# Combining expert outputs: gates applied at the exit from PSUM, and gathers that add onto x inside the DMA

## What is computed

```python
def rms_norm(x, g):
    y = x * rsqrt(mean(x * x, axis=-1) + 1e-6)
    return y * g

for layer in range(2):
    h = rms_norm(x, norm_mix_g[layer])
    x = x + mixer[layer](h)
    h = rms_norm(x, norm_ffn_g[layer])
    x = x + hier_moe(h, ...)
return rms_norm(x, norm_final_g)

def hier_moe(h, ...):            # of each token: 2 experts, each with a gate
    ...
    gate = softmax(top_v) * p_g[:, None]
    expert = g_sel[:, None] * 8 + top_i
    ...
    def expert_block(xb, e):
        return (silu(xb @ w_gate[e]) * (xb @ w_up[e])) @ w_down[e]
    ...
    y = zeros_like(t).at[tok_sorted].add(ybuf[dest] * gate_sorted[:, None])
```

## Time and profile before

| what | us |
|---|---|
| median of 3 runs | 1822.61 (1816.19 to 1827.16) |
| the profiled execution | 1822.49 |
| its span, first to last instruction | 1820.7 |
| VectorE busy in the span | 541.3 |
| TensorE busy in the span | 1421.9 |
| GpSimd busy in the span | 166.1 |

### The profile page before, as it was taken

The page is one execution under the profiler, slowest core; times in us unless marked ns, Lnnn a source line. Parts: engine busy times, 40 slices in busy tenths (PEclk is TensorE's granted clock), DMA queues, the critical chain, the costliest instruction groups (busy, mean ns, idle before and its releaser), DMA issues. The chain is left out here.

```text
span 1820.7 us, 18610 instructions
## 1 busy us (share of the span) xinstructions
PE 1421.9 (78%) x7013; PEld 685.3 (38%) x7013; DVE 541.3 (30%) x1109; ACT 247.1 (14%) x501; POOL 166.1 (9%) x211
## 2 busy tenths in 40 slices
PE   6998757968977877877848977894988878868872
PEld 3443745543333333322313456653333323323330
DVE  6998596231110110110123157324111101101014
ACT  2201322111000000000001035311100000000001
POOL 0007250001000000000010000000000000000002
PEclk9999977978998998998987989995998988988996
DMA  6512405247999999999984200406999999999995
GB/s 227 171 37 29 33 13 217 84 187 286 388 396 399 397 401 403 400 397 404 405 347 154 93 1 1 186 35 266 341 374 405 395 395 402 389 393 407 396 419 189
DMA packets 75026, 494.38 MB, mean 272 GB/s; under 512 B 14704, under 2 KB 21488, under 8 KB 50016
## 3 DMA queue, kind: packets, MB, share of 16 engines
q1 hardware_dynamic: 53984, 440.23, 62.5%
q0 software_dynamic: 9472, 32.32, 5.7%
q10 hardware_dynamic: 11520, 21.15, 3.1%
HBM read 465.88 MB, written 27.79 MB: 271 GB/s over the span
## 5 line engine op out<-in xcount | busy, mean ns | idle before, releaser
L565 PE MATMUL psum<-ring,work 128*64 128x512 f32 x992 | 501.7, 665 | 162.3 <-DMA ring<-in_moe_w_up 159.5
L566 PE MATMUL psum<-ring,work 128*64 128x512 f32 x992 | 502.4, 666 | 0.0
L565 PEld LDWEIGHTS psum<-ring,work 128*64 128x64 f32 x992 | 147.5, 153 | 489.5 <-issue 486.1
L578 PE MATMUL psum<-ring,work 128*64 128x512 f32 x992 | 226.6, 599 | 31.4 <-DVE work L716 31.4
L713 DVE TENSOR_TENSOR work<-work,psum 64x512 f32<-64x512 f32 x64 | 44.1, 690 | 681.9 <-ACT work L670 608.0
L670 ACT ACTIVATE work<-psum 64x512 f32<-64x512 f32 x64 | 37.8, 590 | 879.0 <-PE psum L566 879.0
L566 PEld LDWEIGHTS psum<-ring,work 128*64 128x64 f32 x992 | 147.5, 153 | 0.0
L578 PEld LDWEIGHTS psum<-ring,work 128*64 128x64 f32 x992 | 66.7, 137 | 145.2 <-issue 125.3
L719 DVE COPY work<-psum 128x512 f32<-128x512 f32 x64 | 44.3, 692 | 247.9 <-PE psum L578 247.9
L1495 PE MATMUL psum<-ring,hT 128*128 128x512 f32 x256 | 112.1, 600 | 2.1 <-ACT work L1614 2.1
L862 POOL COPY ints<-ints 64x1 uint32 (+1 forms) x64 | 11.4, 178 | 864.3 <-PE psum L557 816.0
(11 more groups left out here) (341 smaller groups left out, 1415.9 us busy)
## 6 DMA issues: line engine op xcount, KB each, us to landing
ring<-in_moe_w_gate SPq DMA_DIRECT2D x62, 2048.0 KB, 17.7
ring<-in_moe_w_up SPq DMA_DIRECT2D x62, 2048.0 KB, 24.1
ring<-in_moe_w_down SPq DMA_DIRECT2D x62, 2048.0 KB, 24.0
y_dram<-work ACTq DMA_DIRECT2D x128, 128.0 KB, 9.0
ring<-in_hyb_w_in SPq DMA_DIRECT2D x5, 2048.0 KB, 9.7
ring<-in_swa_w_qkv SPq DMA_DIRECT2D x3, 2048.0 KB, 17.9
y_dram<-ones POOLq DMA_DIRECT2D x1, 4096.0 KB, 19.9
ring<-in_hyb_w_out SPq DMA_DIRECT2D x2, 2048.0 KB, 10.6
```

The source lines that it names most:

```text
L565: nc.tensor.matmul(bank[2 + b][0:BLK, :], XT[b][:, c, :], g[:, c, :], start=c == 0, stop=c == KC - 1)
L566: i = nc.tensor.matmul(bank[2 + b][BLK:P, :], XT[b][:, c, :], u[:, c, :], start=c == 0, stop=c == KC - 1)
L578: i = nc.tensor.matmul(bank[6 + b][BLK * hf:BLK * (hf + 1), :], HTE[b][:, c, :], d[:, c, hf * HALF:(hf + 1) * HALF], start=c == 0, stop=c ...
```

## The change

1. The token-number product goes to a second table `BL2`, and `BL1` stays a plain one-hot table of blocks. VectorE multiplies `BL1` with the gates (128x384), and TensorE multiplies places with it into PSUM bank 5, once for each half of the partitions: 16 more matmuls. VectorE copies the result, a gate for every row of every block, to `SLG` (128x48).
2. `dve_y` is a multiplication by the column of `SLG` that belongs to the block, instead of a copy. Inside the loops the column's number is in a register. The rows in `y_dram` are now already times their gates.
3. The 8 gathers go straight onto x: `compute_op=ALU.add` makes the DMA add the row that it fetches onto `xv[:, t, :]`. The order is k=0 of the four tiles, then k=1 of the four tiles, and each of the last four waits until the k=0 gather of the same tile has landed.
4. The 8 multiply-adds of VectorE per layer, the buffers `YK` and the semaphore `x_new` are gone; ScalarE's norm and SyncE's loads wait for the k=1 gathers themselves.

```diff
--- before.py
+++ after.py
@@ -217,7 +217,6 @@
         dve_own, act_own, pool_own = Count("dve_steps"), Count("act_steps"), Count("pool_steps")
         n_sq, n_ms, n_rt, n_h, n_hp, n_ea, n_ed = (Count(n) for n in (
             "norm_squares", "norm_mean", "norm_root", "norm_rows", "norm_transposed", "norm_evac_act", "norm_evac_dve"))
-        x_new = Count("x_updated")
         p_tr, p_ev, c_tr, c_ev = (Count(n) for n in ("s5_rows_transposed", "s5_rows_out", "s5_c_transposed", "s5_c_out"))
         sc_a, sc_b = Count("s5_dve_to_act"), Count("s5_act_to_dve")
         u_mm, u_ea, u_tr, u_ev = (Count(n) for n in ("u_proj", "u_evac", "u_transposed", "u_ready"))
@@ -316,7 +315,6 @@
         HD = [WK[0:BLK, 12288 + 512 * b:12800 + 512 * b] for b in range(2)]
         HTE = [cut(WK, 13312 + 256 * b, 256).rearrange("p (c n) -> p c n", c=HC) for b in range(2)]
         YE = [cut(WK, 13824 + 512 * b, 512) for b in range(2)]
-        YK = [cut(WK, 1024 * i, 1024) for i in range(8)]
 
         W2 = [cut(WK, 4096, SLOT), cut(WK, 0, SLOT), HT[:, :]]
         RT0 = 14848
@@ -350,12 +348,15 @@
         assert 20 + MAXOV + 2 <= 64
         ONES = sb("ones", P)
         gates = rt("gates")
+        BL2 = cut(WK, 12288 + 8 * NBLK, 8 * NBLK)
+        SLG = rt("big")[:, 0:NBLK]
 
         g_lg, g_ex, g_exr, g_A, g_C, g_idx, g_zero, g_wr = (Count(n) for n in (
             "router_logits", "router_to_act", "router_exp", "router_onehots", "router_counts", "router_indices",
             "ones_set", "router_weights_joined"))
         h_st = sem("h_stored")
         g_L, g_Lm, g_sl = Count("router_places"), Count("router_lists_mm"), Count("router_lists")
+        g_G, g_Gm = Count("router_gate_places"), Count("router_gate_lists_mm")
         xg_ld = [sem(f"x_block{b}") for b in range(2)]
         e_stg, e_xt, e_xe, e_gu, e_a, e_h, e_ht, e_he, e_dn, e_y = (sem(n) for n in (
             "blk_index", "blk_x_transposed", "blk_x_evac", "blk_gate_up", "blk_silu", "blk_hidden", "blk_h_transposed",
@@ -388,10 +389,17 @@
             i.then_inc(g_C.s, 1)
 
             pe.wait_ge(g_L.s, l + 1)
-            pl, bl = shp(PL1, 8, BLK), shp(BL1, 8, NBLK)
+            pl, bl, bg = shp(PL1, 8, BLK), shp(BL2, 8, NBLK), shp(BL1, 8, NBLK)
             for a in range(8):
                 i = nc.tensor.matmul(bank[2][0:BLK, 0:NBLK], pl[:, a, :], bl[:, a, :], start=a == 0, stop=a == 7)
             i.then_inc(g_Lm.s, 1)
+
+            pe.wait_ge(g_G.s, l + 1)
+            for hf in range(2):
+                for a in range(8):
+                    i = nc.tensor.matmul(bank[5][BLK * hf:BLK * (hf + 1), 0:NBLK], pl[:, a, :], bg[:, a, :], start=a == 0,
+                                         stop=a == 7)
+            i.then_inc(g_Gm.s, 1)
 
         def act_router(act, l, A_):
             act.wait_ge(g_ex.s, 2 * l + 1)
@@ -524,13 +532,15 @@
             V(tv.tensor_tensor(rt("ob"), rt("ob"), rt("ei"), ALU.add))
             V.sync()
             V(tv.scalar_tensor_tensor(rt("row"), rt("ob"), float(BLK), rt("pos"), ALU.mult, ALU.add))
-            bl = shp(BL1, 8, NBLK)
+            bl, bt = shp(BL1, 8, NBLK), shp(BL2, 8, NBLK)
             V(tv.tensor_tensor(shp(PL1, 8, BLK), ins_dim(rt("pos"), 2, BLK), ins_dim(cst("eid"), 1, 8), ALU.is_equal))
             V(tv.tensor_tensor(bl, ins_dim(rt("ob"), 2, NBLK), ins_dim(cst("eid")[:, 0:NBLK], 1, 8), ALU.is_equal))
             V.sync()
             for k in range(2):
-                V(tv.tensor_tensor(bl[:, NT * k:NT * (k + 1)], bl[:, NT * k:NT * (k + 1)], ins_dim(cst("tok"), 2, NBLK),
+                V(tv.tensor_tensor(bt[:, NT * k:NT * (k + 1)], bl[:, NT * k:NT * (k + 1)], ins_dim(cst("tok"), 2, NBLK),
                                    ALU.mult), g_L if k else None)
+            V.sync()
+            V(tv.tensor_tensor(bl, bl, ins_dim(gates, 2, NBLK), ALU.mult), g_G)
             V(tv.tensor_tensor(rt("cle").rearrange("p (b e) -> p b e", e=NE), ins_dim(rt("inc"), 1, MAXOV + 1),
                                ins_dim(cst("bidx"), 2, NE), ALU.is_le))
             V.sync()
@@ -541,6 +551,8 @@
             V(tv.tensor_copy(SLL, bank[2][0:BLK, 0:NBLK]), g_sl)
             V.sync()
             V(tv.tensor_copy(OVI[:, 1:MAXOV + 2], rt("eov")), g_idx)
+            dve.wait_ge(g_Gm.s, l + 1)
+            V(tv.tensor_copy(SLG, bank[5][:, 0:NBLK]))
             V.sync()
 
         def overflow_blocks(eng, l, body):
@@ -715,8 +727,9 @@
         def dve_he(b, done):
             nc.vector.tensor_copy(HTE[b], bank[4 + b][:, 0:HC * BLK].rearrange("p (c n) -> p c n", c=HC)).then_inc(done, 1)
 
-        def dve_y(b, done):
-            nc.vector.tensor_copy(YE[b], bank[6 + b][:, :]).then_inc(done, 1)
+        def dve_y(b, blk, done):
+            col = SLG[:, blk:blk + 1] if isinstance(blk, int) else SLG[:, bass.ds(blk, 1)]
+            nc.vector.tensor_scalar(YE[b], bank[6 + b][:, :], col, None, ALU.mult).then_inc(done, 1)
 
         def dve_moe(dve, l):
             b0 = NE * l
@@ -737,7 +750,7 @@
                 if l or not (isinstance(e, int) and e < 3):
 
                     dve.wait_ge(y_st[1 - par], 16 * b0 + (e - 3 - (1 - par)) * 16 + 32)
-                dve_y(1 - par, e_y)
+                dve_y(1 - par, e - 1, e_y)
 
             hid(0, 0)
             for e in (1, 2):
@@ -758,7 +771,7 @@
                 dve.wait_ge(o["ht"], j + 1)
                 dve_he(1, o["he"])
                 dve.wait_ge(o["dn"], j + 1)
-                dve_y(1, o["y"])
+                dve_y(1, j + NE, o["y"])
 
             overflow_blocks(dve, l, body)
 
@@ -884,8 +897,11 @@
             for b in range(2):
                 pool.wait_ge(y_st[b], 16 * NE * (l + 1))
             overflow_wait(pool, l, "st", 32)
-            for i in (k * NT + t for t in range(NT) for k in range(2)):
-                pool.indirect_dma_start(YK[i], None, y_dram, bass.IndirectOffsetOnAxis(ROWI[:, i:i + 1], 0)).then_inc(yk_ld[i], 16)
+            for i in range(2 * NT):
+                if i >= NT:
+                    pool.wait_ge(yk_ld[i - NT], 16 * (l + 1))
+                pool.indirect_dma_start(xv[:, i % NT, :], None, y_dram, bass.IndirectOffsetOnAxis(ROWI[:, i:i + 1], 0),
+                                        compute_op=ALU.add).then_inc(yk_ld[i], 16)
 
         def overflow_wait(eng, l, what, each):
 
@@ -895,15 +911,7 @@
 
         def dve_combine(dve, l, V):
             for t in range(NT):
-                for k in range(2):
-                    i = k * NT + t
-                    dve.wait_ge(yk_ld[i], 16 * (l + 1))
-                    V(nc.vector.scalar_tensor_tensor(xv[:, t, :], YK[i], gates[:, i:i + 1], xv[:, t, :], ALU.mult,
-                                                     ALU.add), x_new if k else None)
-                    V.sync()
-                if t:
-                    dve_norm_tile(dve, V, 2 * l + 2, t - 1)
-            dve_norm_tile(dve, V, 2 * l + 2, NT - 1)
+                dve_norm_tile(dve, V, 2 * l + 2, t)
 
         def shp(ap, *dims):
 
@@ -1867,7 +1875,7 @@
                                 bank[a][64 * g:64 * g + 64, :]), done if g and hf else None)
 
         def act_mixer1(act, A_):
-            act_norm(act, A_, 2, lambda e, t: e.wait_ge(x_new.s, t + 1))
+            act_norm(act, A_, 2, lambda e, t: e.wait_ge(yk_ld[NT + t], 16))
             act_norm_evac(act, A_, 2)
             for i in range(4):
                 act.wait_ge(a_q.s, 2 * i + 1)
@@ -1973,7 +1981,8 @@
                 sp.dma_start(Wrows(i, KC), wqkv_v[:, :, 512 * i:512 * i + 512]).then_inc(w_in[i], 16)
 
         def sp_mixer1(sp):
-            sp.wait_ge(x_new.s, NT)
+            for t in range(NT):
+                sp.wait_ge(yk_ld[NT + t], 16)
             sp.dma_start(Wrows(2, KC), wqkv_v[:, :, 1024:1536]).then_inc(w_in[2], 16)
             sp.dma_start(SINK, bass.AP(A["swa_sink"].tensor, 0, [[0, P], [1, AH]])).then_inc(sk_in, 16)
             sp.wait_ge(f_st, 16)
@@ -2071,7 +2080,7 @@
                     act.wait_ge(f_ev.s, 1)
                     act.dma_start(f_dram, FS).then_inc(f_st, 16)
                 act_moe(act, l)
-            act_norm(act, A_, 4, lambda e, t: e.wait_ge(x_new.s, NT + t + 1))
+            act_norm(act, A_, 4, lambda e, t: e.wait_ge(yk_ld[NT + t], 32))
 
         @block.tensor
         def _(pe):
```

## The result

The changed kernel takes **1828.55 us** (median of 8 runs, 1822.97 to 1837.33) against 1819.78 (median of 8 runs) of the kernel before beside it: a ratio of 1.0051, 95% interval 1.0026 to 1.0076, so 4.7 to 13.9 us more. In a later comparison it was 1.0047 [1.0020, 1.0074]. It is slower: the ratio on 1822 us is +9.3 us, about two thirds of the 14.5 that were forecast. The profiled execution took 1827.67 us, its span is 1825.8.

What follows compares the result with a forecast made beforehand. DMA engines were taken to bound the expert loops, VectorE to end late in the combines. Adding gathers +11.1, stores +2.6 and router +0.8 make +14.5 us on 1822.49: 1837 us, own range 1832 to 1841.

Steps and rivals of the forecast that it cites:

- What bounds the kernel, where the change acts: DMA engines bound the expert loops; the change can act only in each layer's combine and in the router.
- The products at the exit: Results' exit from PSUM: 64 copies of 692 ns become products of 690 ns, no difference; at worst 1.4 us in all.
- The router: Gate lists and block-gate product delay the first expert block: 0.7 us in layer 0, some 0.05 per layer, together +0.8 us.
- 5.75 + 8g: Each layer's combine, first gather issue to last scaling, in us; g is one 512 KB gather's time on the DMA engines.
- g = 3.04: Combine: one adding gather takes 3.04 us, middle of two-read cases 2.88 to 3.20, against 1.60 plain; both layers +11.1 us.
- Stores inside the gathers: Layer 1's combine: two tiles' output stores share the DMA engines while later gathers run, 2 x 1.28 = +2.6 us.
- The waits: Combine: waits of the last four gathers for their k=0 gathers do not count of themselves, since DMA work stays queued.
- the wide range over the rivals: Whole kernel: 1810 to 1857 us, from the free add to the slow add's lower end, two in ten left out.
- The free add: Rival for the combine: adding costs the DMA nothing, g = 1.60, -11.1 us, 1811 us; chance 0.22.
- The partial overlap: Rival for the combine: the read of x hides beside the DRAM read, g about 2.2, -0.2 us, 1822 us; chance 0.22.
- The slow add: Rival for the combine: the adding itself is slow, g 4.16 to 4.80, +32 to +43 us, 1855 to 1865; chance 0.13.
- The clock: Rival: 16 more router matmuls raise TensorE's clock before the first expert block, 2.5 us less; chance 1 in 10.

Runs made afterwards that it cites:

- the exit gates alone: Kernel before plus router gate lists and products at the PSUM exit; gathers stay plain in old order, VectorE adds rows onto x: 1821.97 us, ratio 0.9997.
- the kernel without the adds: Changed kernel's order and waits, but gathers copy into buffers and the sum onto x is left out: 1812.16 us, ratio 0.9944.
- with the adds but without the waits: Changed kernel, but each gather adds onto a buffer of its own, so none waits, and x gets nothing: 1831.62 us, ratio 1.0046.
- the bfloat16 run: Changed kernel with eight adding DMAs without indices in place of gathers, rows from a bfloat16 input of zeros: 1812.11 us (one run).
- the adds without the gather: Changed kernel with its eight adding gathers replaced by adding DMAs without indices, same waits: 1834.96 us (one run).

## Why the prediction was right in sign and too high by half

*What bounds the kernel, where the change acts.* Right. With the exit gates alone the time did not move (0.9997), and the table shows the combines as the place.

*The products at the exit, at nothing.* Right on the path. Each took 750 ns, not 690: 0.06 us for the last one of a layer.

*The router, +0.8 us.* Too high. From the cast of the token list to the first block's copy it was 414.30 to 420.84 = 6.54 us, and is 415.93 to 422.51 = 6.58. That is 0.04 us, not 0.7 there and 0.8 in all. The 32 records took 3.23 us instead of 3.9 (16 records take 1.94, the next 16 only 1.29), so the bias ended soon enough: the transposes still waited 0.68 us for the gather, and ScalarE's store, issued at 421.50, was over before they ended.

*5.75 + 8g.* The form held in layer 0: 1.98 to first data, 21.57 of data, 0.89 to the last square, 3.18 for the norm make 27.62. The fixed part is 6.05, with 0.5 more at the start and 0.1 less each at the receipt and the norm. It holds only while g is large; the kernel without the adds shows 21.3 us where it gives 18.6.

*g = 3.04.* **This is the mis-sized term.** Measured 2.70 in the whole stretch, 2.56 in its steady part. The two reads, the mechanism of the forecast, are borne out; their price was not. I added the second read to the 1.60 us of a plain gather. But those 1.60 were not the full rate of the DMA engines: 512 KB at 410 GB/s is 1.28 us, and a plain gather's other 0.32 did not come again in the adding one. Measured is bytes by the full rate: 2 x 512 KB at 410 GB/s are 2.56 us, the steady part. The 398 GB/s of the earlier trace rows would have told it: 2 x 524288 bytes / 398 GB/s = 2.63 us. Over 16 gathers the error is 16 x 0.34 = 5.4 us. Why the plain gathers stay below that rate is not shown. That GpSimd issues too slowly does not explain it alone: in the earlier trace rows the last gather's issue ended at 955.38, and the data flowed on until 958.55.

*Stores inside the gathers, +2.6 us.* Did not come. The first store of layer 1 is issued at 1816.46, but its data flow only from 1818 on:

```profile
1816.46 6.70 SPq L2014 DMA_DIRECT2D out_y<-work  x4
```

```profile
1817.00:1818.00 1.00, 0.00 (x0) 0.00 (x0) 0.93 (x1) 0.88 (x1) 0.00 (x0) 0.50 0.95 217
1818.00:1819.00 1.00, 0.00 (x0) 0.00 (x0) 0.62 (x3) 0.48 (x3) 0.00 (x0) 0.50 1.02 397
```

I had tile 0 scaled 21.0 us after the first issue and the data's end at 25.8. Tile 0 was scaled at 1815.15 + 1.28 - 1794.53 = 21.9, later than I said though g is smaller: its square starts only 17.7 us after the first issue, where 2.5 + 5 x 2.7 would be 16.0, and the table load of 1.28 us holds its norm up by 1.0. And the data ended at 23.5. The store's own way to its first data, 1.5 us, fills the rest. At most the last landing suffered: the last square starts 1.6 us after the data's end, against 0.9 in layer 0.

*The waits, at nothing.* Right: without the adds GpSimd waited 4.7 us and the data stretch stayed at 13.0 us; with the adds but without the waits the combines stayed at 27.7 us.

*The sum.* Forecast +11.1 + 2.6 + 0.8 = +14.5. The combines' part came out at +6.9: 5.4 less by g, 2.6 less by the stores, and 1.2 more by the fixed parts (0.3 in each layer) and the late landing in layer 1. Router and exit add 0.1. The measured +9.3 [4.7, 13.9] holds that 7, and does not hold 14.5. As a time, the forecast's own range of 1832 to 1841 does not hold the median of 1828.55 either; only the wide range over the rivals does, and that it does so is no merit of the sum.

*The rivals.* The free add (1811) is out by g. The partial overlap (g near 2.2) is out as a mechanism: g is 2.56 at least, and in the bfloat16 run the source's bytes count in full, not hidden beside the read of x. The slow add is out. *The clock* brought nothing in the first expert block of the changed kernel, as I held likely: it came to 1.00 about 6 us after the block's first large matmul in both of its traces, as in both of before. But with the same router it came after 2.6 us with the exit gates alone (first large matmul at 421.90, shorter ones from 424.51) and in the adds without the gather, so the rival was no idle one. It also moved elsewhere, where I had not looked (below).

## What to carry to other kernels

Price a DMA that adds by the bytes of both operands at the full rate that the DMA engines show in a long stream (398 to 410 GB/s here), not by adding a read to the time of a transfer that itself runs below that rate. Work taken off an engine is worth no more than the distance to the next late one. Of the 6.5 us between the last data and VectorE's last pair in the earlier trace rows, up to 2.3 were the receipt (no landing took over 6.4 us, so the last gather had landed by 960.8) and 1.3 the last multiply-add, which stands there anyway. The kernel without the adds is only 3 us a layer shorter, and the add's extra read of 8 x 512 KB took 6 to 7 back. And when a stage's parts all become ready at once, what follows them (four norms at 1.9 us, a table load) queues at the end and belongs in the sum.
